# A fused decoder layer on one core: the first operand of the first pair is multiplied without its norm, and the squares are shared with GpSimd

## The reference, cut to what matters

```python
D_MODEL, SEQ, D_FF, EPS = 1024, 1024, 2816, 1e-6

def rmsnorm(x, g):
    x32 = x.astype(jnp.float32)
    y = x32 * lax.rsqrt(jnp.mean(x32 * x32, axis=-1, keepdims=True) + EPS)
    return (y * g.astype(jnp.float32)).astype(x.dtype)

def swiglu(x, w_gate, w_up, w_down):
    return (jax.nn.silu(x @ w_gate) * (x @ w_up)) @ w_down

    x = x + 0.5 * swiglu(rmsnorm(x, ffn1_norm[l]), ffn1_w_gate[l], ffn1_w_up[l], ffn1_w_down[l])
    h = rmsnorm(x, mix_norm[l])
    ...
    x = x + concat(y_swa, y_gla, y_mem) @ w_out[l]
    x = x + 0.5 * swiglu(rmsnorm(x, ffn2_norm[l]), ffn2_w_gate[l], ffn2_w_up[l], ffn2_w_down[l])
```

## Time and profile before

| | |
|---|---|
| time, median of 3 runs | 1685.18 us (1684.99 to 1685.77) |
| time of the profiled execution | 1685.31 us |
| its span (first to last instruction) | 1683.5 us |
| PE busy | 1673.8 us, 99% of the span |
| DVE, ACT, POOL busy | 1112.9, 726.7, 562.5 us |

### The profile page before, as it was taken

One profiled execution on the slowest core, in us unless ns is written; L12 is line 12 of the kernel. 1 busy time (PEld: TensorE's weight loads), 2 busy tenths in 40 slices (PEclk: granted clock), 3 DMA queues, 4 the chain that ended last, 5 costly groups with the idle time before them and its releaser, 6 DMA issues.

```text
span 1683.5 us, 25083 instructions
## 1 busy us (share of the span) xinstructions
PE 1673.8 (99%) x8399; PEld 1373.1 (82%) x8399; DVE 1112.9 (66%) x1574; ACT 726.7 (43%) x1378; POOL 562.5 (33%) x471
## 2 busy tenths in 40 slices
PE   9999999999999999999999999999999999999999
PEld 7888888888888889888766787888888888888887
DVE  7965555555488688458888935985555555569664
ACT  6433333333344465333378723443333333334442
POOL 0544445554130134012267422355444444310000
PEclk9999999999999999999999999999999999999999
DMA  7342222233774432220100223133333222584434
GB/s 215 81 144 94 100 100 93 99 107 114 258 265 145 162 95 88 63 81 20 38 2 2 64 75 137 39 106 107 120 112 110 93 93 106 188 283 148 144 100 163
DMA packets 101790, 191.73 MB, mean 114 GB/s; under 512 B 11539, under 2 KB 14068, under 8 KB 101708
## 3 DMA queue, kind: packets, MB, share of 16 engines
q1 hardware_dynamic: 100624, 188.50, 32.7%
q0 software_dynamic: 848, 2.10, 1.0%
q10 hardware_dynamic: 236, 0.06, 0.0%
HBM read 139.76 MB, written 50.86 MB: 113 GB/s over the span
## 4 chain that ended last, share of the span: by engine, by line
PE 97%; ACT 1%; DVE 1%; DMA 1%; issue 0%; SPq 0%; ACTq 0%; DVEq 0%
PE ps L57 30%; PE ps L59 30%; PE ps L58 30%; PE ps L1856 1%; PE ps L1763 1%; PE ps L1893 1%; PE ps L1841 1%; PE ps L1753 1%; DMA xT<-in_x 1%; ACT Pg L1969 0%; DVE A_T L2088 0%; PE ps L1908 0%; PE ps L1809 0%; PE ps L1879 0%; ACT glu L2004 0%
## 5 line engine op out<-in xcount | busy, mean ns | idle before, releaser
L521 DVE TENSOR_TENSOR ring<-w_raw,ring 128x512 fp32r<-128x512 f32 x240 | 238.0, 1007 | 219.8 <-ACT ring L516 219.5
L57 PE MATMUL ps<-hiT,ring 128*128 128x512 f32 x672 | 261.5, 389 | 0.4 <-issue 0.4
L59 PE MATMUL ps<-hiT,ring 128*128 128x512 f32 x672 | 261.4, 389 | 0.0
L58 PE MATMUL ps<-loT,ring 128*128 128x512 f32 x640 | 249.0, 389 | 0.0
L57 PE MATMUL ps<-down_ring 128*128 128x512 f32 x616 | 239.6, 389 | 0.0
L58 PE MATMUL ps<-down_ring 128*128 128x512 f32 x616 | 239.6, 389 | 0.0
L59 PE MATMUL ps<-down_ring 128*128 128x512 f32 x616 | 239.6, 389 | 0.0
L57 PE MATMUL ps<-hiB,ring 128*128 128x512 f32 x576 | 224.8, 390 | 0.3 <-DVE loB L386 0.3
L59 PE MATMUL ps<-hiB,ring 128*128 128x512 f32 x576 | 224.1, 389 | 0.0
L516 ACT ACTIVATE ring<-w_raw 128x512 fp32r<-128x512 f32 x240 | 150.5, 628 | 169.8 <-PE ps L59 162.1
L895 ACT ACTIVATE down_ring<-down_raw 128x512 fp32r<-128x512 f32 x176 | 108.6, 629 | 223.2 <-DMA down_raw<-act_dram 180.1
(11 more groups left out here) (298 smaller groups left out, 3014.6 us busy)
## 6 DMA issues: line engine op xcount, KB each, us to landing
down_raw<-act_dram SPq DMA_DIRECT2D x154, 256.0 KB, 2.6
w_raw<-in_w_gate SPq DMA_DIRECT2D x88, 256.0 KB, 3.1
w_raw<-in_w_up SPq DMA_DIRECT2D x88, 256.0 KB, 3.2
act_dram<-actT SPq DMA_DIRECT2D x88, 256.0 KB, 2.0
act_dram<-act SPq DMA_DIRECT2D x66, 256.0 KB, 2.0
wd<-in_w_down SPq DMA_DIRECT2D x44, 256.0 KB, 4.8
wd_mirrored<-in_w_down SPq DMA_DIRECT2D x33, 256.0 KB, 4.4
p_raw<-in_w_proj SPq DMA_DIRECT2D x15, 512.0 KB, 3.6
```

The source lines that it names most:

```text
L57: nc.tensor.matmul(out, w_hi, x_hi, start=first, stop=False, skip_group_check=resumed)
L58: nc.tensor.matmul(out, w_hi, x_lo, start=False, stop=False, skip_group_check=resumed)
L59: return nc.tensor.matmul(out, w_lo, x_hi, start=False, stop=last, skip_group_check=resumed)
L521: nc.vector.tensor_tensor(ring[:, e % RING, 1, :], op_source(e), ring[:, e % RING, 0, :].bitcast(F32), ALU.subtract).then_inc(op_ready, 1)
```

## The change

What it does:

- B11 is made without the norm. ACT writes x times gain as its high part (`first_hi`), DVE the low part with one scalar_tensor_tensor (`first_lo`). When units 0 to 3 have been multiplied, DVE multiplies their four PSUM banks by the norm (`first_scale`), and B21 is added into the same banks.
- The second pair needs the normed B11. It is made anew inside `head_vector` as part "B11n": four `prep_norm`, four `split_hi`, four `split_lo`, in the same tiles.
- Of each half's eight squares GpSimd makes four (`POOL_SQUARES`), ACT the other four.
- PE's sums of squares stand in its stream of products: those of half 0 behind the first 24 matmuls of B11, those of half 1 in the middle of B21. `keep_warm` is gone.
- The load order on SP's queue: x piece 0, weights "11", x pieces 1 to 3, weights "21" and "12", x of half 1, weights "22". The identity comes over ACT's queue.

```diff
+SPLIT_ORDER = (HEAD_PARTS[:4] + ("B11n",) + HEAD_PARTS[4:], HEAD_PARTS)
+POOL_SQUARES = 4
...
+        def first_hi(act, m):
+
+            act.wait_ge(x_landed[m // 2], 16)
+            nc.scalar.activation(part_hi_of(0, "B11", m), part(xT, m, 0), ACT.Copy,
+                                 scale=gains[:, 0, m:m + 1]).then_inc(part_hi, 1)
+
+        def first_lo(dve, m):
+            dve.wait_ge(part_hi, part_count(0, "B11", m))
+            nc.vector.scalar_tensor_tensor(out=part_lo_of(0, "B11", m), in0=part(xT, m, 0), scalar=gains[:, 0, m:m + 1],
+                                           in1=part_hi_of(0, "B11", m).bitcast(F32), op0=ALU.mult, op1=ALU.subtract
+                                           ).then_inc(part_ready, 1)
+
+        def first_scale(dve, u):
+
+            bank = ps[:, pair_bank(0, u // 2, u % 2), :]
+            dve.wait_ge(prod_done, u + 1)
+            nc.vector.tensor_tensor(bank, bank, rstd[:, 0:HALF], ALU.mult).then_inc(first_scaled, 1)
...
         def prep_norm(dve, f, h, m):
 
             at, by = scaled_x(f, m, h), rstd[:, h * HALF:(h + 1) * HALF]
-            if f == 0 and h == 0 and m < KK:
-                by = ps[:, BANK_NORM + h, :]
-                if m == 0:
-                    dve.wait_ge(rstd_step, rstd_spread(h))
-            elif m == (KK if f == 0 and h == 0 else 0):
+            if m == (KK if f == 0 and h == 0 else 0):
                 dve.wait_ge(rstd_ready, NHALF * 2 * f + h + 1)
-            if f == 0 and h == 0 and m < KK:
-                dve.wait_ge(x_scaled, m + 1)
-                ins = nc.vector.tensor_tensor(at, at, by, ALU.mult)
-            else:
-                x_in_place(dve, f, h, m)
-                ins = nc.vector.scalar_tensor_tensor(out=at, in0=part(xT, m, h), scalar=gains[:, 2 * f, m:m + 1], in1=by,
-                                                     op0=ALU.mult, op1=ALU.mult)
-            ins.then_inc(x_normed, 1)
+            x_in_place(dve, f, h, m)
+            nc.vector.scalar_tensor_tensor(out=at, in0=part(xT, m, h), scalar=gains[:, 2 * f, m:m + 1], in1=by,
+                                           op0=ALU.mult, op1=ALU.mult).then_inc(x_normed, 1)
...
                 if f == 0 and r == "B11":
-                    pe.wait_ge(op_ready, b.head_op + 2)
                     for k in range(KK):
                         pe.wait_ge(part_ready, part_count(f, r, k))
                         kc = slice(k * P, (k + 1) * P)
                         for u in units[:2]:
+                            pe.wait_ge(op_ready, b.head_op + u + 1)
                             mm = split_product(nc, ps[:, pair_bank(h, 0, u), :], unit_slot(u)[:, 0, kc],
                                                unit_slot(u)[:, 1, kc], part_hi_of(f, r, k), part_lo_of(f, r, k),
                                                k == 0, False, True)
                             if k == KK - 1:
                                 mm.then_inc(prod_done, 1)
-                    pe.wait_ge(x_squared, 2 * KT)
-                    for m in range(3, KT):
-                        mm = tok_sum(1, m, False, m == KT - 1)
-                    mm.then_inc(norm_summed, 1)
+                    tok_sums(pe, 0)
+                    units = units[2:]
+                if f == 0 and r == "B21":
+                    for k in range(KK):
+                        pe.wait_ge(part_ready, part_count(f, r, k))
+                        kc = slice(k * P, (k + 1) * P)
+                        for u in units[:2]:
+                            pe.wait_ge(op_ready, b.head_op + u + 1)
+                            pe.wait_ge(first_scaled, u - 4 + 1)
+                            mm = split_product(nc, ps[:, pair_bank(h, 0, u - 4), :], unit_slot(u)[:, 0, kc],
+                                               unit_slot(u)[:, 1, kc], part_hi_of(f, r, k), part_lo_of(f, r, k),
+                                               False, k == KK - 1, True)
+                            if k == KK - 1:
+                                mm.then_inc(prod_done, 1)
+                        if k == 1:
+                            tok_sums(pe, 1)
+                    rstd_rows(pe, 1)
...
+                    if f == 0 and r == "B21":
+                        pe.wait_ge(first_scaled, u - 4 + 1)
...
+                        if f == 0 and r == "B11" and u == 2 and k == 2:
+                            rstd_rows(pe, 0)
                     mm.then_inc(prod_done, 1)
-                    if f == 0 and r == "B11" and u == 2:
-                        rstd_rows(pe, 1)
...
             hi("B12")
             hi("B22")
+            if f == 0:
+                hi("B11n")
             head_silu(act, f, 0, 0, G11)
             head_silu(act, f, 0, 1, G21)
             hi("T1")
...
             lo("B22")
+            if f == 0:
+                for j in range(KK):
+                    prep_norm(dve, f, 0, j)
             sums(sum_t1)
+            if f == 0:
+                lo("B11n")
...
+        def tok_sums(pe, h):
+
+            pe.wait_ge(x_squared, (KT - POOL_SQUARES) * (h + 1))
+            pe.wait_ge(pool_product, POOL_SQUARES * (h + 1))
+            for m in range(KT):
+                mm = tok_sum(h, m, m == 0, m == KT - 1)
+            mm.then_inc(norm_summed, 1)
...
-            x_sync(sp, 0)
+            x_sync(sp, 0, (0,))
             for x in range(2):
                 load_w(sp, 0, x, "11", 0)
-            sp.dma_start(ident[:], ident_in).then_inc(rel_bias_landed, 16)
-            x_sync(sp, 1)
-            for q in ("21", "12", "22"):
+            x_sync(sp, 0, (1, 2, 3))
+            for q in ("21", "12"):
                 for x in range(2):
                     load_w(sp, 0, x, q, 0)
+            x_sync(sp, 1)
+            for x in range(2):
+                load_w(sp, 0, x, "22", 0)
...
+            for h in range(NHALF):
+                for m in range(POOL_SQUARES):
+                    pool.wait_ge(x_landed[4 * h + m // 2], 16)
+                    nc.gpsimd.tensor_tensor(squares[h][:, m, :], part(xT, m, h), part(xT, m, h), ALU.mult
+                                            ).then_inc(pool_product, 1)
...
+            act.dma_start(ident[:], ident_in).then_inc(rel_bias_landed, 16)
...
 
-            for m in range(KT):
+            act.wait_ge(gains_landed, 16)
+            first_hi(act, 0)
+            ops(0, 0, 1)
+            for m in range(1, KK):
+                first_hi(act, m)
+            for m in range(POOL_SQUARES, KT):
                 square(m, 0)
-            ops(0, 0)
+            ops(0, 2, 3)
             tok_root(act, 0)
-            ops(0, 1)
-            for m in range(3):
-                square(m, 1)
-            split_hi(act, 0, "B11", 0)
-            for j in range(1, KK):
-                split_hi(act, 0, "B11", j)
-                square(2 + j, 1)
-            for m in range(6, KT):
-                square(m, 1)
-            rstd_copy(act, 0)
-            ops(0, 2, 3)
             act.wait_ge(bias_row_summed, 1)
             nc.scalar.activation(bias_row[:], ps[0:SWA_HEADS, BANK_BIAS, 0:ROW], ACT.Copy).then_inc(bias_row_ready, 1)
+            ops(0, 4, 5)
+            rstd_copy(act, 0)
+            for j in range(2):
+                split_hi(act, 0, "B21", j)
+            for m in range(POOL_SQUARES, KT):
+                square(m, 1)
+            for j in range(2, KK):
+                split_hi(act, 0, "B21", j)
+            ops(0, 6, 7)
             tok_root(act, 1)
-            ops(0, 4, 5)
-            hi(0, "B21")
-            ops(0, 6, 7)
             rstd_copy(act, 1)
...
-                    for m in range(KK):
-                        prep_scale(dve, f, m)
+                    first_lo(dve, 0)
+                    ops(0, 1)
+                    for m in range(1, KK):
+                        first_lo(dve, m)
+                    ops(2, 3)
                     tok_recip(dve, 0)
-                    ops(0, 1)
-                    for j in range(KK):
-                        prep_norm(dve, f, 0, j)
-                        if j:
-                            split_lo(dve, f, "B11", j - 1)
-                    split_lo(dve, f, "B11", KK - 1)
-                    ops(2, 3)
+                    ops(4, 5)
+                    for j in range(0, KK, 2):
+                        prep_norm(dve, f, 0, KK + j)
+                        prep_norm(dve, f, 0, KK + j + 1)
+                        for i in (j, j + 1):
+                            if j == 0:
+                                first_scale(dve, i)
+                            split_lo(dve, f, "B21", i)
+                    first_scale(dve, 2)
+                    first_scale(dve, 3)
+                    ops(6, 7)
+                    tok_recip(dve, 1)
+                    return
                 for j in range(KK):
                     prep_norm(dve, f, 0, KK + j)
                     if j:
                         split_lo(dve, f, "B21", j - 1)
-                    elif f == 0:
-                        tok_recip(dve, 1)
                 ops(4)
```

(19 more changed lines are left out.)

38 lines of the change are left out of this document (22 added, 16 removed).

## The result

The changed kernel takes 1695.85 us (median of 6 runs, 1694.64 to 1697.28) against 1685.36 (6 runs, 1684.99 to 1686.15) of the kernel before: a ratio of 1.0061, 95% interval 1.0048 to 1.0074. It is 10.5 us slower; 1693.3 had been forecast. The profiled executions are 1695.41 us, span 1693.3, against 1685.31 and 1683.5, so 9.8 of the 10.1 us between them lie inside the span.

What follows compares the result with a forecast made beforehand. PE is busy 99% of the span, and DVE's list up to L733 was taken as equally tight. 3.7 + 5.1 - 0.7 = 8.1 us on 1685.31 gave 1693.4, so 1693.3 us at the median; range 1687.5 to 1696.5.

Steps and rivals of the forecast that it cites:

- the forecast's own case: Whole kernel: DVE's longer list delays PE at the addition, 1690.5 to 1695 us, chance 0.54.
- half clock in the opening, with x of half 1 late: Opening: PE slow through 24 products and sums, 1695 us, plus late x; upper end of range, 1696.5.
- The bound: Up to L733: DVE's list is as tight as PE's stream, idling 2.1 us in two waits on ACT.
- The opening, +3.7: Before the head's list: DVE starts that list at 34.3 us instead of 30.55, +3.7 us.
- costed at nothing: Given no time: ACT's four more copies, identity on ACT's queue, removed matmuls on ones, later x of half 1.
- The second making, +5.1: Head's list on DVE: remaking B11 takes four scalar_tensor_tensor and four tensor_tensor with nothing to hide beneath, +5.1 us.
- idle -0.7: Head's list on DVE: part of 2.1 us idle time goes as ACT's copies are ready relatively earlier, -0.7 us.
- two of 8 to 9 together: PE waits twice, before the second pair's second product and before the product with T1, 8 to 9 us together.
- After that PE is full again: Behind the wait at L733's bank: PE is full as before and nothing gives time back.
- rival 2: Opening: PE stays at half clock through its first 24 products and the sums, another 1.3 to 2 us, 1695; chance 0.14.
- Rival 1: Opening: the lock between GpSimd and DVE does not bite, head's list starts 3.6 us sooner, 1689.7 us; chance 0.14.
- Rivals 3 and 4: PE's earlier stream decides, 1683.9 us (0.08); half of DVE's added work hidden, plus opening at half clock, 1685 to 1688 (0.10).

Runs made afterwards that it cites:

- e4: Kernel before the change, with eight more operations on DVE where the change remakes B11, results overwritten: 1691.48 us.
- e8: Changed kernel with PE kept busy before its first product, bias matmul later, fewer GpSimd squares, second norming earlier, DVE's first addition ahead of eight operations: 1688.93 us.
- e9: Kernel before the change, with DVE's first addition (L733) put ahead of eight operations: 1690.16 us.
- e10: e8 without the second splitting of B11 (four low parts on DVE, four copies on ACT), outputs not the reference's: 1687.19 us.
- e3: Changed kernel with the four scalar_tensor_tensor of B11's second making moved from the head's list to behind DVE's second reciprocal: 1693.61 us.
- e2: Changed kernel with all eight squares of half 0 on ACT, GpSimd making four only of half 1: 1696.66 us.
- e5: Changed kernel with eight DVE operations (low parts of ring weights and T3) put behind the first addition L773 instead of ahead of it: 1692.40 us.

## Why the prediction was right, point by point

The sign and the mechanism were as forecast: a longer list on DVE, met by PE at the addition. The size was too small: two terms of 2.6 us together were missing, and the others were too large by only 0.8. The measured 1695.85 lies above the 1690.5 to 1695 of the forecast's own case. It lies inside the range because this reached up to 1696.5, for a rival (half clock in the opening, with x of half 1 late) that is not what happened; that part of the fit is luck.

- **The bound.** "DVE's list up to L733 is as tight as PE's stream": right, and shown by e4, where 5.1 us on DVE gave 4.2 at the addition. It is tight further than was said, up to the third pair's addition near 111 us (e8, e9, e10); in the changed kernel it doesn't show, since there the third pair's addition is 8.0 us late (118.17 for 110.14) and PE's product, put back further by its slow stretch, 9.3 (120.40 for 111.11).
- **The opening, +3.7.** Measured +3.2, with its steps off in both directions. First product 8.66 for 8.4, but for another reason: the identity "costed at nothing" gates it. Low parts done at 12.2 for 13.1: three operations took turns, not all, because x's second piece came later than counted on (GpSimd idles 0.91 us for it), and a square of GpSimd's alone takes 1.04 us, not the 1.29 of a sum. The half clock was taken at +1.2; eight products 0.20 longer (not 0.23) are 1.6. Sums through at 17.8 for 19.2, B21 from 21.7 for 23.0. From there 12.1 us for 11.3: the spreading waits in PE's order behind products, so the second gap is 2.27 and not 1.7. Fewer turns than counted and more slow products than counted nearly cancelled.
- **The second making, +5.1, idle -0.7.** Measured 45.66 - 41.60 = 4.06 us for the list, of which one wait of 0.88 is gone: 5.0 and -0.9.
- **PE.** One gap of 9.0 us, not two of 8 to 9 together: the product before, said to wait as well, found its weights ready. "After that PE is full again": right.
- **What was missing.** PE's clock behind its own long wait, 2.0 us. The forecast asked that question of the opening only (its rival 2), and not of the longer pause 65 us later that it forecast itself. The Trainium skill, "TensorE: Matmul & The Clock Gate", section "What's actually happening", has the throttled clock as the resting state; that would have asked for this term, and the trace agrees (granted clock 0.50 from 76 to 80 us, while PE stood still). Then 0.5 us near 471.7, where PE waits once for a down-projection weight that DVE, ACT and a load pass on, and 0.1 behind it; neither was traced further. Of the other runs only e10 loses about as much at the first place (0.4 us), e3 0.2 and the rest nothing, so it is no steady cost of the change.
- **Rivals.** Rival 1, no lock in the opening, is half right (three turns), and e2 shows that it decides nothing as long as the identity and the clock hold the products. Rival 2 came true for eight of the 24 products. Rivals 3 and 4 are excluded: the addition is at 79.4, where they needed 72 to 76.

In sum +3.2 +5.0 -0.9 +2.0 +0.6 = 9.9 for the 9.8 us of the spans; +8.1 had been forecast.

## What to carry to other kernels

Starting the bottleneck engine 7 us sooner is worth nothing when another engine's list meets it later with as little slack; count that list from its start to the place where the two meet, and then on to the next such place, before adding an operation to it or moving one forward. A pause of PE of several microseconds has a second price behind it, at half clock, and belongs in the sum wherever the pause stands. What stands ahead of the meeting point counts in full (4.8 us for eight operations moved, e5), but an operation moved so far ahead that it waits for PE loses the same time (e9).
